# Unread turns of the identity at eleven places of TensorE's order, and products of ones ahead of its first work, in a two-block transformer kernel

## What is computed

```python
for layer in range(2):                      # first block
    x = x + 0.5 * swiglu(rmsnorm(x))        # 1024 -> 2*2816 -> 1024
    x = x + mixer(rmsnorm(x))               # layer 0: stick-breaking attention and spatial gate; layer 1: MLA, 16 heads
    x = x + memory_cross_attention(x, mem)  # 4 heads of 256
    x = x + 0.5 * swiglu(rmsnorm(x))
for i in range(2):                          # second block
    h = layer_norm(alpha * h + 0.5 * swiglu(h))
    mix = conv and S5 state space (i = 0), or index-selected attention, 8 heads of 128 (i = 1)
    h = layer_norm(alpha * h + mix)
    h = layer_norm(alpha * h + 0.5 * swiglu(h))
    h = h + (p[i] @ w_proj[i]) * sigmoid(h @ w_gate[i])
```

## Time and profile before

| | |
|---|---|
| median of 3 runs | 2282.71 us (2280.7 to 2287.32) |
| the profiled execution, its own time | 2281.97 us |
| its span, first to last instruction | 2280.2 us |
| TensorE busy with matmuls | 2217.6 us, 97% of the span |
| VectorE, ScalarE, GpSimd busy | 1429.7, 1125.8, 188.1 us |
| mean granted TensorE clock | 0.992 |
| chain that ended last | TensorE 85%, VectorE 10%, ScalarE 3% |

### The profile page before, as it was taken

The page is one execution under the profiler, slowest core; times in us unless marked ns, Lnnn a source line. Parts: engine busy times, 40 slices in busy tenths (PEclk is TensorE's granted clock), DMA queues, the critical chain, the costliest instruction groups (busy, mean ns, idle before and its releaser), DMA issues.

```text
span 2280.2 us, 25958 instructions
## 1 busy us (share of the span) xinstructions
PE 2217.6 (97%) x10482; PEld 1827.0 (80%) x10482; DVE 1429.7 (63%) x1923; ACT 1125.8 (49%) x1678; POOL 188.1 (8%) x219
## 2 busy tenths in 40 slices
PE   8999999999999999999999999979999999999999
PEld 6888877888888887778888887657887888777887
DVE  6655665655565577656556876886556555576556
ACT  6545565545454457555435443334444444364443
POOL 0000000000000020000001970530000000010000
PEclk9999999999999999999999999999999999999999
DMA  8656534566565563336656565425665666425553
GB/s 288 186 186 219 159 112 149 175 185 186 194 211 185 175 207 94 114 122 196 185 188 204 185 185 173 141 84 189 185 190 193 189 186 188 163 93 192 185 188 126
DMA packets 111144, 396.55 MB, mean 174 GB/s; under 512 B 13232, under 2 KB 14000, under 8 KB 110896
## 3 DMA queue, kind: packets, MB, share of 16 engines
q1 hardware_dynamic: 111024, 394.90, 54.3%
HBM read 393.80 MB, written 1.05 MB: 173 GB/s over the span
## 4 chain that ended last, share of the span: by engine, by line
PE 85%; DVE 10%; ACT 3%; issue 1%; DMA 0%; POOL 0%; SPq 0%; DVEq 0%; ACTq 0%; POOLq 0%
PE bank L567 26%; PE bank L569 26%; PE bank L568 26%; DVE wlo L1730 3%; PE bank L615 2%; PE bank L626 2%; PE bank L682 1%; PE bank L668 1%; ACT whi L1149 1%; DVE bank L2312 0%; DVE bank L2315 0%; DVE ab_B L2319 0%; PE bank L657 0%; DVE ds_work L2432 0%; DVE together L1866 0%
## 5 line engine op out<-in xcount | busy, mean ns | idle before, releaser
L1730 DVE TENSOR_TENSOR wlo<-raw,whi 128x1024 fp32r<-128x1024 f32 (+2 forms) x718 | 877.8, 1260 | 234.0 <-ACT whi L1149 232.7
L1149 ACT ACTIVATE whi<-raw 128x1024 fp32r<-128x1024 f32 (+2 forms) x718 | 721.4, 1049 | 177.8 <-DMA raw<-in_w_w 89.8
L567 PE MATMUL bank<-whi,XH 128*128 128x512 f32 (+2 forms) x1840 | 729.7, 397 | 7.0 <-DVE wlo L1730 3.0
L569 PE MATMUL bank<-whi,XL 128*128 128x512 f32 (+2 forms) x1840 | 716.5, 389 | 0.0
L568 PE MATMUL bank<-wlo,XH 128*128 128x512 f32 (+2 forms) x1840 | 715.6, 389 | 0.0
L567 PEld LDWEIGHTS bank<-whi,XH 128*128 128x128 f32 x1840 | 348.7, 190 | 79.8 <-issue 8.7
L569 PEld LDWEIGHTS bank<-whi,XL 128*128 128x128 f32 x1840 | 348.0, 189 | 72.1
L568 PEld LDWEIGHTS bank<-wlo,XH 128*128 128x128 f32 x1840 | 348.9, 190 | 66.1
L567 PE MATMUL bank<-whi,HH 128*128 128x512 f32 x704 | 276.5, 393 | 0.0
L569 PE MATMUL bank<-whi,HL 128*128 128x512 f32 x704 | 274.9, 390 | 0.0
L568 PE MATMUL bank<-wlo,HH 128*128 128x512 f32 x704 | 274.6, 390 | 0.0
(11 more groups left out here) (405 smaller groups left out, 2031.1 us busy)
## 6 DMA issues: line engine op xcount, KB each, us to landing
raw<-in_w_w SPq DMA_DIRECT2D x264, 512.0 KB, 3.5
raw<-in_w_gu_pre SPq DMA_DIRECT2D x88, 512.0 KB, 3.6
raw<-in_w_gu_post SPq DMA_DIRECT2D x88, 512.0 KB, 3.6
raw<-in_w_dn_pre SPq DMA_DIRECT2D x44, 512.0 KB, 3.5
raw<-in_w_dn_post SPq DMA_DIRECT2D x44, 512.0 KB, 3.6
raw<-in_w_x_kv SPq DMA_DIRECT2D x32, 512.0 KB, 4.0
raw<-in_w_sbg_in SPq DMA_DIRECT2D x20, 512.0 KB, 4.3
raw<-in_w_x_q SPq DMA_DIRECT2D x16, 512.0 KB, 4.7
```

Source lines behind the costliest of these rows:

```text
L567: pe.e.matmul(o, xh, hi[:, k, :], start=kt == 0, stop=False)
L569: m = pe.e.matmul(o, xl, hi[:, k, :], start=False, stop=kt == kts - 1)
L1149: act.e.activation(whi[v % SLOTS][:, 0:n], raw[v % SLOTS][:, 0:n], ACT.Copy).then_inc(*hi_ok.did(v))
L1730: dve.e.tensor_tensor(wlo[v % SLOTS][:, 0:n], raw[v % SLOTS][:, 0:n], whi[v % SLOTS][:, 0:n].bitcast(F32), ALU.subtract).then_inc(*lo_ok.d ...
```

## The change

`pe_busy` issues n turns of the identity by itself into a bank; nobody reads them. Without a bank it takes the next scratch bank, waits for that bank's last reader as any other user does, and leaves the bank with no reader. At the head of the program the same function multiplies a tile of ones (GpSimd writes it first) into bank 0. These are 209 instructions: 186 turns and 23 products. The eleven places of turns are the keys `ev` to `ds` of the table; `xm` and `ml_out` are reached twice, `glu` has four counts and `ds` two.

```diff
+BUSY = {"first": 13, "product": 10, "ev": 14, "xm": 9, "xk": 11, "ml": 4, "ml_out": 13, "state": 12, "glu": (8, 15, 7, 9), "gated": 15,
+        "ln01": 18, "raw1": 8, "ds": (7, 14)}
...
+        def pe_busy(n, b=None, src=ident):
+            if b is None:
+                b = banks.scratch("busy")
+                pe_open(b)
+                b.open_after = []
+            else:
+                pe_open(b)
+            for _ in range(n):
+                if src is ident:
+                    pe.e.transpose(b.t[:, 0:128], src, src)
+                else:
+                    pe.e.matmul(b.t[:, 0:128], src, src, start=True, stop=True)
...
         def pe_piece(key, c, t, kts=4):
+            if key == "raw1" and (c, t) == (0, 0):
+                pe_busy(BUSY["raw1"])
...
         def pe_attend(name, scores, ready, values, vready):
+                if name[:2] == "xm" and i == 2:
+                    pe_busy(BUSY["xm"])
+                if name == "ml" and i == 12:
+                    pe_busy(BUSY["ml"])
+                if name == "ds" and i in (2, 3):
+                    pe_busy(BUSY["ds"][i - 2])
                 if 2 <= i < heads + 2:
...
         def pe_xk_turn(l, c):
+            if (l, c) == (1, 0):
+                pe_busy(BUSY["xk"])
...
             for t in range(2):
                 pe_piece("ev", 1, t)
             pe_later.add([(t, ("piece", "ev", 0, t)) for t in range(2)])
+            pe_busy(BUSY["ev"])
...
+            def attended(kt, t):
+                if (kt, t) == (4, 0):
+                    pe_busy(BUSY["ml_out"])
+                return lhs_of("ml")(kt, t)
+            for _ in pe_run("mla_out", attended, lambda c, t: [(dve_ok, ("acc", "xm1", c, t))], pieces("xm1"), tail=True):
...
         def pe_ab_state(i):
+            if i == 7:
+                pe_busy(BUSY["state"])
             b = banks.scratch(("abs", i))
...
                     u = index["glu", kt // 2]
+                    pe_busy(BUSY["glu"][kt], banks.all[6])
...
             banks.spare = [4, 5, 6, 7]
+            pe_busy(BUSY["gated"], banks.all[6])
             half(2)
...
                 if t == 1:
+                    pe_busy(BUSY["ln01"], banks.all[6])
                     for x in pe_later.take((None, 0)):
...
         def pe_program():
+            ones = H[0][3][:, 0, 0, 0:128]
+            pe.wait_ge(pool_ok, "ones")
+            pe_busy(BUSY["first"], banks.all[0], ones)
...
+            pe_busy(BUSY["product"], banks.all[0], ones)
             for l in range(2):
...
         def pool_program():
+            pool.e.memset(H[0][3][:, 0, 0, 0:128], 1.0).then_inc(*pool_ok.did("ones"))
```

More of the change, by code:

```diff
@@ L885, in pe_mla @@
             pe_ok.mark(("open", "xm1"))
-            for _ in pe_run("mla_out", lhs_of("ml"), lambda c, t: [(dve_ok, ("acc", "xm1", c, t))], pieces("xm1"), tail=True):
+            def attended(kt, t):
[3 more added lines that the diff above has]
+            for _ in pe_run("mla_out", attended, lambda c, t: [(dve_ok, ("acc", "xm1", c, t))], pieces("xm1"), tail=True):
                 pass
```

## The result

The changed kernel takes **2292.59 us**, median of six runs (2290.68 to 2293.72), against 2284.16 us for the kernel before (six runs, 2279.71 to 2287.32). The ratio on record is 1.0043, 95% interval 1.0032 to 1.0054 (the quotient of the two medians is 1.0037): slower, by about 0.4%. The forecast was 2290.0 us in a range of 2279 to 2297. The profiled execution spans 2291.0 us against 2280.2, 10.8 more.

The account below looks back on a forecast made before the run. TensorE, busy 97% of the span and carrying 85% of the last-ending chain, was taken as the bound. Gains at the start and filled waits against delays elsewhere summed to +8.0 us on 2281.97: 2290.0 us, range 2279 to 2297.

Parts of the forecast that it names:

- `xm`: At both `xm`, the turn of head 0 now waits for the weights of head 1: +0.4 us each, +0.9 together.
- "So turns count as work for the clock here": From 871.35 to 875.1 us TensorE does only turns and the clock stays at 1.00, so turns hold it high.
- Rival 3: Turns do not count for the clock: 4.6 us at `ml_out`, `gated` and `ln01` not won, 2294.6 us; chance 0.08.
- `ml`, "The low stretch stays", +2.7: Score of head 12 starts 3.1 us later; the half-clock stretch remains, partly in idle time: +2.7 us, between 0 and +3.1.
- `state`, +1.8: 12 turns run behind the bank's release, 1.3 us or 2.6 at the low clock, with VectorE the chain: +1.8 us.
- `glu`, +2.7: Gate products wait until `s_tt` is read in bank 6, then 30 turns and a low clock: +2.7 us, +1.3 to +5.
- `gated` and `ln01`, -3.0: 15 and 18 turns fit into waits, removing the half-clock stretches at 1524.5 and 1541.6: -3.0 us together.
- `ds`, +1.8: At the second `ds`, 14 turns run behind ScalarE's copy, 1.5 us or 3.0 in the remaining half-clock stretch: +1.8 us.
- The start, -0.8: Products of ones raise the clock before the first real product; third unit then waits for `wlo`: -0.8 us, -1.9 to 0.
- Rival 1: Bank waits are swallowed, all five half-clock stretches and the start are won: -8.8 us, 2273.2 us; chance 0.12.
- a fall by over 8 us: TensorE's total idle time down by over 8 us was named as a sign that the forecast is wrong.
- Rival 2: Later waits partly absorb the delays, shrinking +13.4 us to about 6: 2283 us, no difference; chance 0.25.

Follow-up runs that it names:

- experiment 1: The change's bank takings and waits, but no turn and no product of ones, against the kernel before: 2293.19 us, ratio 1.0042.
- experiment 3: Only the products of ones and the turns of the first `ml_out`, `gated` and `ln01`, against the kernel before: 2277.51 us, ratio 0.9975.
- experiment 11: experiment 3 plus 14 turns at the second `ds`; `ml_out` and `ds` turns in an unheld bank; against the kernel before: 2277.5 us, ratio 0.9977.
- experiment 10: Only the products of ones at the start, against the kernel before: 2282.14 us, ratio 0.9999.
- experiment 8: experiment 3 without the 18 turns of `ln01`, against the kernel before: 2279.17 us, ratio 0.9994.
- experiment 2: All turns of the change, written to the next scratch bank without taking it from the round, against the kernel before: 2286.43 us, ratio 1.0015.
- experiment 4: Turns only at the low-clock stretches, ahead of the wait and in banks nobody reads, against the kernel before: 2277.24 us, ratio 0.9975.
- experiment 5: experiment 4 less four `ml` turns and the first `ds`, plus turns at `ev` and both `xm`, against the kernel before: 2276.65 us, ratio 0.9981.
- experiment 9: The whole change without the 4 turns of `ml`, against the kernel before: 2287.45 us, ratio 1.0022.
- experiment 6: Only the 4 turns of `ml`, their bank taken from the round, against the kernel before: 2289.18 us, ratio 1.0035.

## Why the prediction was right, and where its terms were off

The forecast, slower by some 7 to 8 us because of where the turns stand, came true: 2292.59 against 2290.0. Both sides of its mechanism are shown: experiment 1 has a cost without the turns, experiments 3 and 11 the gain without the cost.

That the sum came so near is in part luck. In the profile of after, `ml`, `state` and `glu` cost 3.6 us more than forecast, and the start with `gated` and `ln01` won 1.8 less; against that `ds` cost 1.4 less, and 1.2 were won at `c_in`, where the change does nothing. The split between banks and turns was off as well: the two terms that need no turn, `ml` and `xm`, come to 3.6 us in the sum, and the banks without the turns measured 9.6, some 5 of it by the clock (estimate of experiment 1), for which the prediction had no term.

- **"So turns count as work for the clock here"**: right. One profile does not show it, since the clock also stayed high behind a wait that nothing filled (experiment 10). All the profiles and the means do: behind `ml_out` the clock stayed high in all eight profiles with turns in the wait and fell in four of five without, behind `gated` the same, and behind `ln01` it stayed high in five of seven with turns and fell in all six without. The mean clock is 0.995 in experiment 3 against 0.992, and 0.994 in the change against 0.990 in experiment 1, where only the turns and the products of ones are taken out. Rival 3 is out. The Trainium skill, "TensorE: Matmul & The Clock Gate", Part 4 (PE-mode transpose), by which rival 3 would have been true, does not agree with this; the measurement decides.
- **`ml`, "The low stretch stays", +2.7**: the wait was right to 0.1 us (2.5 us ahead of the score, released by `ml_ol`), the term was not: 4.7. The step that failed took a low stretch of 3.4 us that partly falls into idle time. It was 6.8 us, began with the late score and lay wholly on work of TensorE. 3.4 us more at the low level are 1.7 us, which with the delay of 3.1 makes the 4.7. The delay itself was worked out rightly: the score starts 5.3 us later than before, of which 2.2 were there ahead of the place.
- **`state`, +1.8**: 2.9 in the profile, for the same reason: 6.8 us at the low level instead of 3.4. **`glu`, +2.7**: 3.2 in the profile, 3.3 alone. The working beside the term gives 3.2 (1.5 and 1.7) and not the 2.7 that went into the sum; the bounds given hold it.
- **`ev`, `xk`, the second `ml_out`**: 0.9, 1.2 and 1.4 as worked out. **`xm`**: 0.3 for 0.4.
- **`gated` and `ln01`, -3.0**: `gated` has -1.5 in the profile of after, as forecast; `ln01` has -0.2 there, but the runs (experiment 8) give it 1.7 or more. Here the prediction's term was nearer than the profile of after. VectorE's later waits do take back a part; the median does not show that they take all.
- **`ds`, +1.8**: the turns are paid (1.6), but the low stretch at 2022.9, which the prediction had kept, did not fall, so +0.4. That is not the turns' doing for certain: in experiment 2 they stand at the same place and it fell, and in experiment 3 it did not fall without them.
- **The start, -0.8**: 0.3 to 0.7 in the profiles, nothing in the median. VectorE's `wlo` came 0.3 us later in the profile of after, the range's other end.
- **Rival 1** needs slack behind `ml`, `glu` and `state`, and the delays of `ml` and `state` were paid in full; idle time of TensorE (waits over 0.2 us) did fall, from 57.4 us in 47 to 46.7 in 49, while the kernel got slower. The text had named a fall by over 8 us as a sign against the forecast, and that sign was badly chosen: filled waits are idle time less and nothing gained, except by the clock. More than half of the fall, 5.9 us, lies in the first 20 us, where the products of ones stand. **Rival 2** is seen in small only, 0.3 us behind `ml_out`.

## What to carry to other kernels

Filler work belongs ahead of a wait and into a bank that is free and in no round; then it cost nothing that could be measured and mostly held the clock, here 4 to 6 us of 2284. The same filler in a bank of the round costs through what it displaces: four turns of 0.5 us together cost 3 to 8 us, and where the banks were taken with not one turn in them, the cost stayed. Where a clock moves, compare medians of several executions: the profiled execution of experiment 10 was 6 us below the median of its own kernel.

## What the runs showed of the hardware

- **Behind the same wait the granted clock falls in one execution and not in another.** The wait of 2.08 us at `ml_out`: low in before and in experiment 1, high in experiment 10. The wait of 2.02 us at `ev`: high in before, low in experiments 3, 4 and 10. The 75 runs of the kernel before in the three groups lie between 2277.47 and 2288.82 us, with mean clocks from 0.990 to 0.995.
- **Transposes by the identity that nobody reads hold the clock, mostly.** 13 to 18 of them in a wait of 2.1 to 2.8 us kept it at 1.00 behind the wait in 21 of 23 cases; without them it fell in 14 of 16. The two that failed are both at `ln01`, in experiments 2 and 5.
- **With the waits filled the time is mostly steadier.** Experiment 3 spans 3.0 us over nine runs, experiment 11 3.1 over 11, experiment 2 3.4 over 12, experiment 5 3.6 over 11, the change itself 3.0 over six (experiment 4, with one run 5 us above the others, 6.6, and experiment 9 5.4 over seven); the kernel before 7.6 to 10.4 over 23 to 27. Experiments 1 and 6, which fill nothing, span 4.2 and 3.9 over only five runs each.
- **A delay can double a low stretch.** At `ml`, 3.4 us at the low level became 6.8 in the change and in experiments 1 and 6, each time with the score waiting some 2.5 us. In the other ten profiles, where it waits less, the stretch lasted 3.4 us in four and was not there in six.
